# Leaving out four unused pad tiles between the SBUF tiles of a decoder-layer kernel

## The reference, cut to what matters

```python
D_MODEL, SEQ, D_FF = 1024, 256, 2816
def swiglu(h, w_gate, w_up, w_down):
    return (jax.nn.silu(h @ w_gate) * (h @ w_up)) @ w_down
...
x = x + 0.5 * swiglu(rms_norm(x, norm_ffn1[l]), ffn1_gate[l], ffn1_up[l], ffn1_down[l])
h = rms_norm(x, norm_mix[l])
proj = h @ w_in[l]                                   # 1024 x 5120
y_a = moba_attention(...); y_b = rwkv7_time_mix(h, rb, kb, vb, ...)
merged = jax.nn.sigmoid(ga) * (y_a @ proj_a[l]) + jax.nn.sigmoid(gb) * (y_b @ proj_b[l])
x = x + merged @ w_out[l]
x = x + 0.5 * swiglu(rms_norm(x, norm_ffn2[l]), ffn2_gate[l], ffn2_up[l], ffn2_down[l])
...
return rms_norm(x, norm_final)
```

## Time and profile before

| | |
|---|---|
| median of 3 runs | 647.07 us (646.22 to 648.45) |
| the profiled execution's own time | 647.07 us |
| its span, first to last instruction | 645.2 us |
| TensorE matmuls, busy | 629.1 us, 98% |
| VectorE | 424.4 us, 66% |
| ScalarE | 296.0 us, 46% |
| GpSimd | 93.8 us, 15% |
| read from HBM | 103.5 MB, 162 GB/s |
| granted TensorE clock | 0.999 of 2.4 GHz |

### The profile page before, as it was taken

One profiled execution on the slowest core, in us unless ns is written; L12 is line 12 of the kernel. 1 busy time (PEld: TensorE's weight loads), 2 busy tenths in 40 slices (PEclk: granted clock), 3 DMA queues, 4 the chain that ended last, 5 costly groups with the idle time before them and its releaser, 6 DMA issues.

```text
span 645.2 us, 15471 instructions
## 1 busy us (share of the span) xinstructions
PE 629.1 (98%) x6726; PEld 614.7 (95%) x6726; DVE 424.4 (66%) x487; ACT 296.0 (46%) x337; POOL 93.8 (15%) x95
## 2 busy tenths in 40 slices
PE   7899999999999999999998999999999999999996
PEld 7799999999999999999987889999999999999996
DVE  5866787664556369958994337876866666665662
ACT  6544554443334274425664544544544444443341
POOL 1216600000113000020004424005000000000120
PEclk9999999999999999999999999999999999999999
DMA  8686655555555336584232222356466666555541
GB/s 268 191 258 216 189 179 178 180 168 188 173 179 193 103 132 193 186 182 127 99 131 69 68 85 77 112 188 198 146 186 191 195 195 195 182 163 196 165 141 65
DMA packets 100607, 105.37 MB, mean 163 GB/s; under 512 B 2196, under 2 KB 98684, under 8 KB 100564
## 3 DMA queue, kind: packets, MB, share of 16 engines
q1 hardware_dynamic: 99348, 101.45, 49.1%
q0 software_dynamic: 1056, 3.02, 2.2%
q10 hardware_dynamic: 160, 0.27, 0.1%
HBM read 103.48 MB, written 1.25 MB: 162 GB/s over the span
## 4 chain that ended last, share of the span: by engine, by line
PE 91%; DVE 6%; ACT 1%; issue 1%; DMA 0%; DVEq 0%; ACTq 0%
PE two L1408 26%; PE two L1409 25%; PE two L1410 25%; PE two L1404 11%; DVE w_lo L879 2%; DVE hlo_f L898 1%; PE two L1664 1%; PE two L1665 1%; PE two L1666 1%; DVE w_lo L889 0%; PE two L1807 0%; DVE x L1017 0%; DMA cst<-in_consts 0%; ACT KK L767 0%; DVE rstd L916 0%
## 5 line engine op out<-in xcount | busy, mean ns | idle before, releaser
L525 ACT ACTIVATE w_hi<-w_raw 128x2048 fp32r<-128x2048 f32 (+1 forms) x88 | 166.2, 1888 | 259.1 <-PE two L1410 231.7
L879 DVE TENSOR_TENSOR w_lo<-w_raw,w_hi 128x2048 fp32r<-128x2048 f32 (+1 forms) x88 | 203.7, 2315 | 89.2 <-ACT w_hi L525 88.8
L1408 PE MATMUL two<-hlo_f,w_hi 128*128 128x256 f32 x656 | 183.8, 280 | 2.3 <-DVE w_lo L879 2.3
L1409 PE MATMUL two<-hhi_f,w_lo 128*128 128x256 f32 x656 | 183.3, 279 | 0.0
L1410 PE MATMUL two<-hhi_f,w_hi 128*128 128x256 f32 x656 | 182.6, 278 | 0.0
L1408 PEld LDWEIGHTS two<-hlo_f,w_hi 128*128 128x128 f32 x656 | 123.2, 188 | 3.4 <-DVE w_lo L879 3.4
L1409 PEld LDWEIGHTS two<-hhi_f,w_lo 128*128 128x128 f32 x656 | 123.3, 188 | 0.0
L1410 PEld LDWEIGHTS two<-hhi_f,w_hi 128*128 128x128 f32 x656 | 123.3, 188 | 0.0
L1408 PE MATMUL two<-hid_lo_t,w_hi 128*128 128x256 f32 x352 | 100.0, 284 | 0.0
L1409 PE MATMUL two<-hid_hi_t,w_lo 128*128 128x256 f32 x352 | 99.6, 283 | 0.0
L1410 PE MATMUL two<-hid_hi_t,w_hi 128*128 128x256 f32 x352 | 99.6, 283 | 0.0
(11 more groups left out here) (327 smaller groups left out, 963.4 us busy)
## 6 DMA issues: line engine op xcount, KB each, us to landing
w_raw<-in_ffn_up SPq DMA_DIRECT2D x22, 1024.0 KB, 5.3
w_raw<-in_ffn_gate SPq DMA_DIRECT2D x21, 1024.0 KB, 5.3
w_raw<-in_w_in SPq DMA_DIRECT2D x20, 1024.0 KB, 5.1
w_raw<-in_ffn_down SPq DMA_DIRECT2D x16, 896.0 KB, 4.9
w_raw<-in_ffn_down SPq DMA_DIRECT2D x8, 1024.0 KB, 5.1
w_raw<-in_w_out SPq DMA_DIRECT2D x4, 1024.0 KB, 5.7
w_raw<-in_proj_a SPq DMA_DIRECT2D x4, 512.0 KB, 3.5
w_raw<-in_proj_b SPq DMA_DIRECT2D x4, 512.0 KB, 4.4
```

The costliest lines, as they stand in the source:

```text
L525: nc.scalar.activation(whi[slot][:, 0:kts], raw[slot][:, 0:kts], ACT.Copy).then_inc(sg["hi_ready"], 1)
L879: nc.vector.tensor_tensor(wlo[slot][:, 0:kts], raw[slot][:, 0:kts], whi[slot][:, 0:kts].bitcast(F32), ALU.subtract).then_inc(sg["lo_ready" ...
L1408: mm(dst, whi[slot][:, k_, cols], xl, start=start, stop=False)
L1409: mm(dst, wlo[slot][:, k_, cols], xh, start=False, stop=False)
```

## The change

Four lines that allocate a tile are taken out. No instruction is added, removed, moved or given another shape: on all five engines the order, the operands' tiles and the waits of the built program are the same as before. What differs is the address of the tiles behind each pad.

```diff
         with ExitStack() as sc:
             h_f = sb("h_f", [P, KD, T], scope=sc)
-            sb("pad_f", [P, 48], scope=sc)
             hhi_f = sb("hhi_f", [P, KD, T], F32R, scope=sc)
             hlo_f = sb("hlo_f", [P, KD, T], F32R, scope=sc)
             silu = sb("silu", [P, 2, T], scope=sc)
             prod = sb("prod", [P, 2, T], scope=sc)
-            sb("pad_hid", [P, 56], scope=sc)
             hid_hi = sb("hid_hi_t", [P, FT, T], F32R, scope=sc)
             hid_lo = sb("hid_lo_t", [P, FT, T], F32R, scope=sc)
             out_tok = sb("out_tok", [P, 2, D], scope=sc)
...
             with ExitStack() as sc:
-                mb("pad_y", [P, 8], scope=sc)
                 ybhi = mb("ybhi", [P, HT, T], F32R, scope=sc)
                 yblo = mb("yblo", [P, HT, T], F32R, scope=sc)
                 pa = mb("pa", [P, 2, 2, T], scope=sc)
                 mg = mb("mg", [P, KD, T], scope=sc)
-                mb("pad_m", [P, 32], scope=sc)
                 mhi = mb("mhi", [P, KD, T], F32R, scope=sc)
                 mlo = mb("mlo", [P, KD, T], F32R, scope=sc)
```

## The result

The changed kernel takes 653.67 us (median of 4 runs, 652.64 to 654.25) against 646.64 us (645.47 to 648.45) for the kernel before: a ratio of 1.0104, 95% interval 1.0077 to 1.0133. It is **slower by 1.0%**. The forecast was no change; the time lies 0.7 us above the end of the range, next to the 652.5 us of rival 2.

A forecast was written before the change was run, and what follows sets the result against it. TensorE's matmuls were taken as the bound, so time is nearly their number times their pitch. Against 647.07 us the terms +0.4 + 1.5 - 1.9 - 0.1 summed to -0.1 us, giving 647.0 us, range 643.5 to 653.0.

The forecast's parts named there:

- rival 2: SwiGLU stages: offset 96 is bad, gate and up fall to 120.0 ns, down gains nothing; +5.4 us, 652.5 us; chance 0.28.
- What bounds the kernel, and the pitch as the only way in: Whole kernel: TensorE matmuls busy 98% of the span; the change acts through matmul pitch or operations touching moved tiles.
- The distance of the two operands sets the pitch: TensorE matmuls: moving and next stationary operand interfere most at the same place modulo 128 bytes; pitches 3% apart.
- I take 118.2, next to the row at 224: SwiGLU stages at new offset 96: pitch 118.2 ns, near the swapped v chunks' 118.0 at 224; bounds 116.7 and 120.0.
- Term `pad_f`: SwiGLU gate and up, offset 32 to 96, pitch to 118.2 ns: +0.4 us in block 1, +1.5 us in block 2.
- Term `pad_hid`: Both SwiGLU down products, 1056 matmuls, from 120.0 to 118.2 ns: -1.9 us (-3.5 to 0).
- Term `pad_y` and `pad_m`: Projection b and output product, 96 and 192 matmuls moved to offset 160: -0.1 us (-0.4 to +0.3).
- VectorE, ScalarE, DMA at 0: Operations and transfers on moved tiles: VectorE shifts of 10 ns at most, covered by TensorE; DMA 0 to +0.3 us; taken as 0.
- rival 4: Whole kernel: addresses do nothing, the down product is slow by its own form; 647.1 us; chance 0.07.

The follow-up runs named there:

- e7: Kernel before with 8 unused float32 ahead of out_tok, so only out_tok, x_tok and vec_rows move, by 32 bytes: 647.28 us, ratio 1.0003.
- e3: Kernel before without pad_f, pad_hid cut to 40, so only SwiGLU gate and up change offset, 32 to 96: 652.82 us, ratio 1.0093.
- e4: Changed kernel with 64 unused bytes ahead of w_raw, so every tile stands 64 bytes higher at unchanged offsets: 653.86 us, ratio 1.0098 to the kernel before.
- e5: Kernel before with weights 64 bytes higher and hhi_f, hid_hi_t in place, offsets 32 to 224 and 0 to 192: 646.05 us, ratio 0.9980.
- c2: Changed kernel with a pad_f of 24 ahead of hhi_f, both SwiGLU stages at offset 192: 636.1 us, ratio 0.9819 to the kernel before.
- c7: Changed kernel with a pad_f of 88 ahead of hhi_f, both SwiGLU stages at offset 448: 640.5 us, ratio 0.9899 to the kernel before.
- e2: Kernel before without pad_y and pad_m alone, SwiGLU tiles where they were: 647.37 us, ratio 1.0009.
- c3: Changed kernel with a pad_f of 40 ahead of hhi_f, both SwiGLU stages at offset 0: 653.2 us, ratio 1.0098 to the kernel before.
- c4: Changed kernel with a pad_f of 8 ahead of hhi_f, both SwiGLU stages at offset 128: 648.8 us, ratio 1.0021 to the kernel before.

## Why the prediction was wrong, step by step

- **What bounds the kernel, and the pitch as the only way in**: right as far as the change goes. The span's 6.7 us are 5.4 us of pitch and 1.2 us of a late landing that `e7` did not tie to the change; the VectorE operations of rows 10 changed by 10 ns at most (`hid_lo_t` from 684 to 694 ns).
- **The distance of the two operands sets the pitch**: right as a cause, shown by `e3`, `e4` and `e5`. It does not set it alone: at several offsets a stage can have either of two pitches. That a stage "keeps it" is right only up to a pause (`c2`, `c7`, `e5`).
- **"I take 118.2, next to the row at 224"**: this step failed. The pitch at offset 96 is 120.0 ns. It rested on the guess that 96 and 224 are alike because they are alike modulo 128. The curve has 118.3 at 224, so the row of the swapped chunks was a good guide to 224, and 224 no guide to 96. The neighbours modulo 256, which I had named (64 and 128), are no guide either: in the SwiGLU stages they have 117.8 and 118.7, and both lie below the 120.0 between them. The row of 128 in the prediction, 120.0 ns in the low-rank stage, would have given the right number, but by luck, as the same stretch of that stage has 118.6 in the changed kernel at the same offset. The curve isn't smooth, and a value between its points can't be read off.
- **Term `pad_f`**: +1.9 us forecast, +5.4 us measured, by the working of rival 2 (2.1 + 3.3), against the one profiled execution before. Gate and up 1 of the same addresses stood at 116.7 ns in `e2` and `e7`; against such an execution the loss would be 1968 x 3.3 = 6.5 us, an estimate. The ratios of `e3`, `c3`, `e4` and the change come to 6.0 to 6.7 us, which lies nearer to this. So the medians can be had from the pitch, without the 1.2 us of the late landing.
- **Term `pad_hid`**: -1.9 us forecast, 0 measured. Offset 0 and offset 96 have the same 120.0 ns.
- **Term `pad_y` and `pad_m`**: -0.1 us forecast; `e2` has +0.6 us with an interval from -0.5 to +1.6: 0 within what it tells.
- **VectorE, ScalarE, DMA at 0**: held (`e7` for the token tiles).
- **Rival 2** gave 652.5 us for this very pitch, and the medians are 652.8 (`e3`), 653.2 (`c3`), 653.7 (the change) and 653.9 (`e4`). The range ended at 653.0: it took in the pitch but left no room for what differs between executions, although the runs shown went up to 1.4 us over their median. That, too, was a term to add.

The Trainium skill's sentence that "PE and ACT never wait on anyone" (SBUF — State Buffer, "Who interferes with whom") was weighed in rival 4. The sentence is about other engines, and no run here bears on that. The same section calls the two read ports of TensorE independent, and there the runs disagree: equal matmuls take 113.4 to 120.0 ns by the distance of their two operands. Where the two reads would meet no run shows.

## What to carry to other kernels

In a kernel bound by dense matmuls that each bring a new stationary operand, the place of the tiles is a thing to tune: read the pitch of each stage from the starts of its matmuls, and where equal shapes differ, try the eight distances of 32 bytes within 256 before rewriting anything. Where a product has more than one stationary operand, look at the distance of each, as `w_hi` and `w_lo` both count. Measure each place instead of reasoning from a neighbour, and look at the profile of each, since a place with two pitches gives a median that depends on which stages happened to fall well.

## What the runs showed of the hardware that was not expected

- The pitch of a [128 x 128] by [128 x 256] float32r matmul with its own weight load goes from 113.4 to 120.0 ns, 5.8%, with the distance of the operands modulo 256 bytes. In the SwiGLU stages 0 and 96 are the worst of the eight, and 192 is the best.
- A dense stretch keeps one of a few pitches as long as nothing interrupts it, and can change it, in either direction, at a pause in which a step takes 0.2 to 0.4 us instead of 0.12. Seen were 116.7 or 117.8 ns at 32, 113.3 or 117.8 at 64, 192 and 448, 117.4 or 118.7 at 160 (and 120.0 in one chunk of projection b of the changed kernel), and at 128 118.7 in `c4` and 120.0 in a stretch of the low-rank stage of the kernel before. In the large products only one was seen at 0, 96 and 224. Gate and up 1 of the kernel before and of `e2` have the same addresses and 117.8 and 116.7 ns.
- In 8 of the 17 profiled executions (`c3` and `e7` among them) the granted clock fell for a while behind the wait that ends at the first loop, at 26 to 28 us. TensorE in `e7_token_tiles_up_32`, which waited for 1.6 us up to 26.2 us:

```profile
20.00:26.00 6.00, 4.61 (x34) 1.00 0.57 178
26.00:28.00 2.00, 1.76 (x8) 0.54 0.28 35
28.00:30.00 2.00, 2.00 (x13) 0.60 1.02 356
30.00:35.00 5.00, 5.00 (x45) 1.00 0.88 281
```

The first loop's matmuls began there at a pitch of 0.21 us, the clock's lower level of 1.2 GHz, and its 960 matmuls took 113.6 us at a later pitch of 116.7 ns, 1.6 us more than 960 x 116.7 ns. The profiled executions of the kernel before and of the changed one had a clock of 1.00 throughout those stretches, behind the same wait. Such a fall may be much of the spread of the times; that is argued and not shown. Of the 82 runs of the kernel before that stand beside the experiments and have a mean granted clock of 0.994 or more, the 29 with 0.997 or more have a median of 646.2 us, and the 53 below it 647.6 us.
